# Gated delta rule in four chunks of 128 tokens, with a seventh level of the triangular inverse

## The reference

```
a_mat = where(tril_strict, (k*beta) @ k.T * decay, 0)        # inside one chunk
t_mat = inverse(eye + a_mat)                                 # unit lower triangular
u = t_mat @ (v*beta);  w = t_mat @ (k*beta*exp(gcum))
attn = where(tril, q @ k.T * decay, 0)
for each chunk:                                              # one after the other
    v_new = u - w @ state
    o     = (q*exp(gcum)) @ state + attn @ v_new
    state = state * exp(g_last) + k_tail.T @ v_new
```

## Time and profile before

| | |
|---|---|
| timed runs, median (lowest to highest) | 2641.55 us (2640.49 to 2644.19), 3 runs |
| profiled execution, span from first to last instruction | 2636.5 us; the profile gives no other time of it |
| PE busy | 97% of the span, 15565 MATMUL instructions |
| DVE, ACT, POOL busy | 49%, 24%, 12% |
| one chain (pair i = 1) | 500.30 to 591.80 us, 91.5 us |
| the four chains | 409.0 to 777.5 us |

### The profile page before, as it was taken

The page is one execution under the profiler, slowest core; times in us unless marked ns, Lnnn a source line. Parts: engine busy times, 40 slices in busy tenths (PEclk is TensorE's granted clock), DMA queues, the critical chain, the costliest instruction groups (busy, mean ns, idle before and its releaser), DMA issues.

```text
span 2636.5 us, 38190 instructions
## 1 busy us (share of the span) xinstructions
PE 2565.0 (97%) x15565; PEld 1758.4 (67%) x15565; DVE 1289.6 (49%) x2857; ACT 628.8 (24%) x1152; POOL 323.4 (12%) x315
## 2 busy tenths in 40 slices
PE   8999989999999999999999999999999999999998
PEld 4777757887885745444444446688864575888887
DVE  2255665766641012000024945676765665777733
ACT  1146543323321213011011144212110022121201
POOL 0222124444442400000001000000000000000000
PEclk9999999999999999999999999999999999999999
DMA  5211111111113222444423110222223212222222
GB/s 196 77 52 49 50 63 50 45 38 50 50 49 128 94 79 82 173 172 163 162 77 128 52 61 33 87 81 88 88 96 112 96 35 80 81 96 80 88 88 80
DMA packets 32519, 227.39 MB, mean 86 GB/s; under 512 B 3552, under 2 KB 4192, under 8 KB 6112
## 3 DMA queue, kind: packets, MB, share of 16 engines
q1 hardware_dynamic: 30384, 219.50, 23.7%
q10 hardware_dynamic: 1968, 5.51, 0.6%
HBM read 222.90 MB, written 2.10 MB: 85 GB/s over the span
## 4 chain that ended last, share of the span: by engine, by line
PE 92%; DVE 4%; ACT 2%; issue 1%; POOL 0%; DMA 0%; ACTq 0%; DVEq 0%; POOLq 0%
PE psum L404 90%; PE psum L902 1%; DVE work L1602 0%; PE psum L2810 0%; PE psum L1251 0%; POOL ring L1444 0%; PE psum L2471 0%; ACT work L2864 0%; DVE work L1055 0%; DMA mixT<-x_dram 0%; PE psum L3908 0%; PE psum L2146 0%; PE psum L1994 0%; DVE mixT L1147 0%; ACT work L968 0%
## 5 line engine op out<-in xcount | busy, mean ns | idle before, releaser
L404 PE MATMUL psum<-hT,ring 128*128 128x256 f32 (+2 forms) x2872 | 542.7, 369 | 8.4 <-issue 3.7
L404 PEld LDWEIGHTS psum<-hT,ring 128*128 128x128 f32 (+1 forms) x2872 | 373.5, 161 | 138.5 <-issue 96.7
L404 PE MATMUL psum<-work,ring 128*128 128x512 f32 (+1 forms) x1176 | 404.9, 496 | 5.3 <-ACT work L3736 2.4
L404 PEld LDWEIGHTS psum<-work,ring 128*128 128x128 f32 x1176 | 221.7, 190 | 168.7 <-issue 146.6
L404 PE MATMUL psum<-xT,ring 128*128 128x256 f32 (+2 forms) x1184 | 293.0, 398 | 8.4 <-ACT work L1384 4.3
L404 PE MATMUL psum<-work,mixT 128*128 128x256 f32 (+2 forms) x1332 | 289.3, 379 | 1.2 <-DVE mixT L3951 0.7
L404 PE MATMUL psum<-work 32*32 32x32 f32 (+8 forms) x5126 | 263.0, 247 | 13.7 <-issue 10.3
L404 PEld LDWEIGHTS psum<-work,mixT 128*128 128x128 f32 (+1 forms) x1332 | 232.1, 182 | 47.6 <-issue 16.4
L404 PEld LDWEIGHTS psum<-work 32*32 32x32 f32 (+3 forms) x5126 | 208.9, 123 | 75.4 <-issue 55.8
L404 PEld LDWEIGHTS psum<-xT,ring 128*128 128x128 f32 (+1 forms) x1184 | 209.8, 187 | 62.0 <-issue 25.1
L404 PE MATMUL psum<-ring,work 128*128 (+1 forms) x568 | 247.0, 593 | 0.6 <-DVE work L3031 0.6
(11 more groups left out here) (477 smaller groups left out, 2772.3 us busy)
## 6 DMA issues: line engine op xcount, KB each, us to landing
ring<-stream_dram SPq DMA_DIRECT2D x204, 1024.0 KB, 4.8
con<-consts_dram SPq DMA_DIRECT2D x1, 2953.0 KB, 13.5
mixT<-x_dram ACTq DMA_DIRECT2D x4, 512.0 KB, 6.4
work<-x_dram ACTq DMA_DIRECT2D x4, 512.0 KB, 6.4
out_dram<-mixT SPq DMA_DIRECT2D x4, 512.0 KB, 3.5
work<-p_dram ACTq DMA_DIRECT2D x1, 512.0 KB, 4.2
con<-ssm_dram ACTq DMA_DIRECT2D x1, 512.0 KB, 3.6
vec<-vecs_dram SPq DMA_DIRECT2D x1, 378.0 KB, 5.6
```

The costliest lines, as they stand in the source:

```text
L404: ins = self.eng.matmul(out, lhsT, rhs, start=start, stop=stop)
```

## The change

The chunk gets 128 tokens, so that a block of 128 holds one chunk. The masks, the running sum and the last decay of a chunk follow from the constant. The loop has 4 rounds instead of 8. All products in it have 128 columns. A seventh level (n = 6) joins the two halves of 64 rows of a block, with products of 64 x 64 by 64 columns (`half_ax`, `half_prod`), four for each head in each of its two bursts. For it level 5 also makes the lower left part of the plain (not transposed) inverse of the upper half: four more products a head on one 32 x 32 tile. `own_blocks` has three more small steps a head, `update` at level 5 one more. The projection products are dealt out anew: 5 and 4 in level 6, 4 before chunk 0, then 5, and 3 and 4 in each half of chunks 1 and 2, 112 as before. `u` now begins after product 88 and chunk 0 after product 92. On ACT `split_last_act` goes ahead of the SiLU of tile K0. On DVE the two halves of a tap tile stand before and behind each state.

```diff
-DH, DD, CH = 8, 128, 64
+DH, DD, CH = 8, 128, 128
@@ Chain, Pair
+                self.half_ax, self.half_prod = (self.A[:, 2 * P * n:2 * P * n + 2 * P].rearrange("p (b n) -> p b n", b=NB)
+                                                for n in range(2))
+                self.half_x = [self.vT[:, s, 2 * P:4 * P].rearrange("p (b n) -> p b n", b=NB) for s in range(2)]
+        CHUNKS, LEVELS = T // CH, 7
+        UPPER, LOWER = slice(0, 64), slice(64, P)
@@ chain_pe, level 5 and after it
+                        for b in range(NB):
+                            e.mm(by_part(h.x_prod)[PARTS[1], b, :], d.xt[s][PARTS[1], b, :], d.prod[s][PARTS[1], b, :])
                         ins = part_pairs(e, h.prod_xt, lambda b, lo, hi: (lo, d.prod[s][hi, b, :], d.xt[s][hi, b, :]))
...
             for s, h in enumerate(H):
                 e.eng.wait_ge(S["xt"], level_nth(i, 5, s))
+                for b in range(NB):
+                    ins = e.mm(h.half_ax[LOWER, b, :], blk(h.aT, b)[UPPER, LOWER], d.half_x[s][UPPER, b, :])
+                ins.then_inc(S["ax"], 1)
+            split.some(e, 5)
+            for s, h in enumerate(H):
+                e.eng.wait_ge(S["prod"], level_nth(i, 6, s))
+                for b in range(NB):
+                    ins = e.mm(h.half_prod[UPPER, b, :], d.half_x[s][LOWER, b, :], blk(h.xinvT, b)[LOWER, LOWER])
+                ins.then_inc(S["prod_xt"], 1)
+            split.some(e, 4)
+            for s, h in enumerate(H):
+                e.eng.wait_ge(S["xt"], level_nth(i, 6, s))
                 four(e, h.A, lambda b: (blk(h.xinvT, b), blk(h.v_b, b))).then_inc(S["u"], 1)
...
-            for c in range(T // CH):
+            for c in range(CHUNKS):
...
-                        e.mm(h.A[:, 0:P], blk(h.wT, b), h.state).then_inc(S["w_state"], 1)
-                        e.mm(h.B[:, at], h.state, h.qdT[:, at], True, False)
-                    if c < 7:
-                        split.some(e, 2)
+                        e.mm(h.A[:, 0:P], blk(h.wT, c), h.state).then_inc(S["w_state"], 1)
+                        e.mm(blk(h.B, c), h.state, blk(h.qdT, c), True, False)
+                    if c < CHUNKS - 1:
+                        split.some(e, 3)
...
-                if c < 7:
-                    split.some(e, 4 if c == 0 else 2)
+                if c < CHUNKS - 1:
+                    split.some(e, 5 if c == 0 else 4)
@@ chain_act
+            split_last_act(e, i + 1, K1)
             if more:
                 tapped_act(e, i + 1, K0)
-            split_last_act(e, i + 1, K1)
@@ chain_dve: product, update, own_blocks
+                    ins = nc.vector.tensor_copy(d.half_x[s][LOWER, :, :], h.half_ax[LOWER, :, :])
...
+                    nc.vector.tensor_scalar(d.half_x[s][PARTS[1], :, PARTS[0]], by_part(h.x_prod)[PARTS[1], :, :], -1.0, None, ALU.mult)
...
+                    ins = nc.vector.tensor_scalar(by_block(h.xinvT)[UPPER, :, LOWER], h.half_prod[UPPER, :, :], -1.0, None, ALU.mult)
...
+                nc.vector.memset(d.half_x[s][PARTS[0], :, PARTS[1]], 0.0)
+                for r in PARTS[0:2]:
+                    nc.vector.tensor_copy(d.half_x[s][r, :, r], d.x[s][r, :, :])
@@ chain_dve: the loop over chunks
+                if c == CHUNKS - 1:
+                    continue
+                if more:
+                    tapped_dve(e, i + 1, (V0, K1, V1)[c], 0, 2)
 ...
-                if more and c < 6:
-                    tapped_dve(e, i + 1, (V0, K1, V1)[c // 2], 2 * (c % 2), 2 * (c % 2) + 2)
+                if more:
+                    tapped_dve(e, i + 1, (V0, K1, V1)[c], 2, 4)
```

More of the change, by code:

```diff
@@ L1219, in level_nth, with state_nth @@
         def level_nth(i, n, s):
-            return (6 * i + n) * 2 + s + 1
+            return (LEVELS * i + n) * 2 + s + 1
         def chunk_nth(i, c, s):
-            return (T // CH * i + c) * 2 + s + 1
+            return (CHUNKS * i + c) * 2 + s + 1
+        def state_nth(i, c, s):
+            return ((CHUNKS - 1) * i + c) * 2 + s + 1
         def tapped(i, t):
@@ L1683, in chain_pe @@
             split.some(e, 4)
-            for c in range(T // CH):
-                b, lo = c // 2, (c % 2) * CH
-                r = slice(lo, lo + CH)
-                at = slice(CH * c, CH * c + CH)
+            for c in range(CHUNKS):
                 if c > 0:
@@ L1692, in chain_pe @@
                             e.eng.wait_ge(S["qd"], nth(i, s))
-                        e.eng.wait_ge(S["state"], chunk_nth(i, c - 1, s) - 2 * i)
-                        e.mm(h.A[:, 0:P], blk(h.wT, b), h.state).then_inc(S["w_state"], 1)
-                        e.mm(h.B[:, at], h.state, h.qdT[:, at], True, False)
-                    if c < 7:
-                        split.some(e, 2)
+                        e.eng.wait_ge(S["state"], state_nth(i, c - 1, s))
+                        e.mm(h.A[:, 0:P], blk(h.wT, c), h.state).then_inc(S["w_state"], 1)
+                        e.mm(blk(h.B, c), h.state, blk(h.qdT, c), True, False)
+                    if c < CHUNKS - 1:
+                        split.some(e, 3)
                 for s, h in enumerate(H):
@@ L1702, in chain_pe @@
                         e.eng.wait_ge(S["attn"], nth(i, s))
-                    if c < 7:
-                        e.mm(h.A[:, P:2 * P], blk(h.k_tail, b), v).then_inc(S["k_vnew"], 1)
-                    ins = e.mm(h.B[:, at], v, blk(h.attnT, b)[:, r], c == 0, True)
-                    if c == T // CH - 1:
+                    if c < CHUNKS - 1:
+                        e.mm(h.A[:, P:2 * P], blk(h.k_tail, c), v).then_inc(S["k_vnew"], 1)
+                    ins = e.mm(blk(h.B, c), v, blk(h.attnT, c), c == 0, True)
+                    if c == CHUNKS - 1:
                         ins.then_inc(S["o_whole"], 1)
-                if c < 7:
-                    split.some(e, 4 if c == 0 else 2)
+                if c < CHUNKS - 1:
+                    split.some(e, 5 if c == 0 else 4)
         def delta_pe(e):
@@ L1871, in product @@
                     ins = nc.vector.tensor_tensor(d.prod[s], by_part(h.ax), bc1(C("level")[:, 32 * n:32 * n + 32], NB), ALU.mult)
-                else:
+                elif n == 5:
                     for hi in PARTS[1::2]:
                         ins = nc.vector.tensor_copy(d.prod[s][hi, :, :], by_part(h.ax)[hi, :, :])
+                else:
+                    ins = nc.vector.tensor_copy(d.half_x[s][LOWER, :, :], h.half_ax[LOWER, :, :])
                 ins.then_inc(S["prod"], 1)
@@ L1919, in chain_dve @@
                 nc.vector.tensor_tensor(d.xt[s], bc1(C("eye32"), NB), by_part(h.prod_xt), ALU.subtract).then_inc(S["xt"], 1)
-            for n in range(1, 6):
+            for n in range(1, LEVELS):
                 for s, h in enumerate(H):
@@ L1951, in chain_dve @@
                         e.eng.wait_ge(S["u_out"], nth(i, s))
-                        nc.vector.tensor_copy(h.vnew[r, 0, :], blk(h.u, b)[r, :]).then_inc(S["vnew"], 1)
+                        nc.vector.tensor_copy(h.vnew[:, 0, :], blk(h.u, 0)).then_inc(S["vnew"], 1)
                     else:
-                        e.eng.wait_ge(S["w_state"], (7 * i + c - 1) * 2 + s + 1)
-                        nc.vector.tensor_tensor(h.vnew[r, c % 2, :], blk(h.u, b)[r, :], h.A[r, 0:P], ALU.subtract)\
+                        e.eng.wait_ge(S["w_state"], state_nth(i, c - 1, s))
@@ L1956, in chain_dve @@
+                        nc.vector.tensor_tensor(h.vnew[:, c % 2, :], blk(h.u, c), h.A[:, 0:P], ALU.subtract)\
                             .then_inc(S["vnew"], 1)
[L1957 to L1967, removed]
@@ L1968, in chain_dve @@
-                if more and c < 6:
-                    tapped_dve(e, i + 1, (V0, K1, V1)[c // 2], 2 * (c % 2), 2 * (c % 2) + 2)
+                if c == CHUNKS - 1:
+                    continue
+                if more:
+                    tapped_dve(e, i + 1, (V0, K1, V1)[c], 0, 2)
+                for s, h in enumerate(H):
+                    e.eng.wait_ge(S["k_vnew"], state_nth(i, c, s))
+                    if c == 0:
+                        ins = nc.vector.tensor_copy(h.state, h.A[:, P:2 * P])
+                    else:
+                        e.eng.wait_ge(S["state"], state_nth(i, c - 1, s))
+                        ins = nc.vector.scalar_tensor_tensor(out=h.state, in0=h.state,
+                                                             scalar=h.eg[:, CH * c + CH - 1:CH * c + CH],
+                                                             in1=h.A[:, P:2 * P], op0=ALU.mult, op1=ALU.add)
+                    ins.then_inc(S["state"], 1)
```

6 lines of the change are left out of this document (3 added, 3 removed).

## The result

The changed kernel takes 2624.17 us (median of 4 executions, 2619.89 to 2626.36); the kernel before took 2641.02 beside it (4 executions, 2635.05 to 2644.19). The ratio is 0.994, with a 95% interval of 0.9925 to 0.9955: 0.6% faster. The profiled execution has a span of 2624.5 us and took 2626.36, so 1.9 us lie around the span; 12.0 us of it are gone from the span of before (2636.5).

The account below looks back on a forecast made before the run. PE, busy 97% of the span, was taken as the bound. A pair: -7.2 + 0.6 + 2.4 + 2.2 = -2.0; four pairs -8.0, plus 1.5 for DVE waits, gives -6.5 us: 2641.55 to 2635, range 2627 to 2644.

Parts of the forecast that it names:

- Removed: 32 products of 0.225 a pair: Loop over chunks on PE: 13 products a head instead of 29, so 7.2 us less a pair.
- Level 5, 0.6 a pair: PE, 8 added products a pair on one 32 x 32 tile at 0.075 each: 0.6 us, bounds 0.2 to 1.8.
- Level 6, 2.4 a pair: PE, 16 products of 0.125 a pair plus 0.4 for changes of array shape: 2.4 us, bounds 1.6 to 4.0.
- The wait at product 92, 2.2 a pair in all four: Ahead of chunk 0, PE waits for POOL's sum, queued behind ACT's copies of `u` and `w`: 2.2 us, bounds 1.5 to 3.0.
- DVE, +0.5 in three pairs: PE waits for DVE 0.3 us after level 5's `update` and 0.2 us for taps at the loop's end, in three pairs.
- The base: Starting time: profiled span 2636.5 us to about 2630; median 2641.55, with 5 us more around it, to 2635.
- PE's "issue" gaps stay as they are: Four chains: 11.1 us in 8 PE gaps without known releaser; the forecast sum had no term for them.
- Rival (c): Added small bursts: PE runs short of instructions, one more 2.7 us gap a pair, +4.3 to +6.4 us in all; chance 0.12.

Follow-up runs that it names:

- second profile: Both kernels run and profiled again with no edit: the kernel before 1.0005, the changed kernel 0.9946 of the kernel before.
- shift of 128: 128 PE instructions (32 one-column products) added at the start of `load_pe` in both kernels: before 0.9943, changed 0.9933 of the unshifted kernel before.
- shift 0: Both kernels with no PE instructions added at the start: before 1, changed 0.9946 (five rounds).
- 64: 64 PE instructions (16 one-column products) added at the start of both kernels: before 0.9934, changed 0.9951 of the unshifted kernel before.
- 192: 192 PE instructions added at the start of both kernels: before 0.9964, changed 0.9937 of the unshifted kernel before.
- sixteen traces: All profiles of this case: both kernels, repeats, and follow-up kernels with shifted lists, ACT's copy moved or only the loop's part; ratios 0.9885 to 1.0005.
- four shifted forms: The kernel before with 64, 128, 192 or 256 PE instructions added at its start: 0.9934, 0.9943, 0.9964 and 0.9986.
- four starts: Each kernel with 0, 64, 128 and 192 PE instructions added at its start: mean ratio 0.9960 before, 0.9942 changed, 0.9901 changed with ACT's copy moved ahead.
- shift of 256: 256 PE instructions (64 one-column products) added at the start of the kernel before: 0.9986 of it unshifted.

## Why the prediction was wrong

The prediction's mechanism held and its sum nearly did; the step that failed is one that has no term in it. Its own steps, in order:

- *Removed: 32 products of 0.225 a pair.* Held. The half-rounds of after follow each other without holes, 2.19 us from 577.52 to 579.71 where half a round of four products (0.90) and three projection products (1.29) stand (weight loads of after):

```profile
577.52 0.41 PEld L404 LDWEIGHTS psum<-work 128*128 128x128 f32 x2
...
579.71 0.41 PEld L404 LDWEIGHTS psum<-work 128*128 128x128 f32 x2
```

- *Level 5, 0.6 a pair.* Too high: 24 products in 0.84 us where 16 took 0.63 is 0.21, the lower bound. The rule of 0.075 for each product on one tile, got from bursts that were spread evenly, didn't hold for a burst that is longer on one tile. Four pairs: 1.6 us of the miss.
- *Level 6, 2.4 a pair.* Held: 1.07 for 8 products is 0.13 each (0.125 taken), and 0.2 for the change of shape. The loads start 0.058 apart (16 from 561.03 to 561.90, two a product), all on one row group. The Trainium skill ("TensorE: Matmul & The Clock Gate", section "Part 3: Packing small matmuls") has such loads wait for the products in flight; a load of 53 ns by that page and a product taken to be as long, one behind the other, would put these rows 0.107 apart (an estimate from the page). The trace doesn't agree: 0.058.
- *The wait at product 92, 2.2 a pair in all four.* Held: 574.14 - 570.82 = 3.32, less 1.29 for three products, is 2.0; PE idle 1.8, four times. Taking away its cause ended the four waits, 7.1 us of idle PE, where 8.4 had been forecast.
- *DVE, +0.5 in three pairs.* About right, and small: at `half_ax` the products of the two heads stand apart in two pairs, so that the burst takes 1.37 and 1.46 us where it takes 1.14 in the others (the second profile shows 0.5 us of idle PE there in one pair). Beside this PE waits 0.4 us at level 5's last burst in one pair (in all four at a shift of 128, 1.5 in all), and at the end of the last pair 2.0 instead of 1.2. No wait on taps is seen at the end of the loop.
- *The base.* Taken as 5 us between the span and the median, from two numbers that belonged to different executions. Where an execution's span and time are both known, 1.9 lie between.
- *What was taken for granted: that PE's "issue" gaps stay as they are.* This failed. In the span they went from 15.2 to 6.7 us, 8.5 us for which the sum has no term. Rival (c) had them, as "the gaps, never explained", and asked only whether new bursts would add some. They hang on the count of instructions ahead of them. The edit shortened the list by 128 and so moved every seam behind the chains by half a piece, to the end of the kernel.

The terms for the chains, then: -6.5 as forecast, -1.6 for level 5, -4.4 for the gaps (11.1 to 6.7), and +1.7 for the clock. For the last, the windows of before and then of after (columns PE, its clock, DMA share, GB/s):

```profile
412.00:502.00 90.00, 85.97 (x1374) 0.98 0.14 47
502.00:593.00 91.00, 88.83 (x1396) 1.00 0.14 48
```

```profile
412.00:502.00 90.00, 84.53 (x1370) 0.98 0.14 48
502.00:593.00 91.00, 87.24 (x1381) 0.98 0.14 48
```

A mean of 0.98 over 90 us is a stretch at the lower level, 1.2 GHz, which costs about 1.7 us. Before had one, behind the gap of 2.1 us at 457 us; after has that one, behind 1.5 us at 456, and one more in pair 1, behind 1.8 at 552. Together -10.8, and -10.6 was measured. At a shift of 128, with as much of gaps in both and no such stretch, the same sum is -6.5 - 1.6 + 1.1 (for the waits at level 5's last burst, three more than at shift 0), so -7.0, against -5.9.

So near a sum as the first is in part luck, as the other pairs of profiles show. Take the chains from the first 32x32 product of pair 0 to their end as above, and from the difference of the two kernels the difference of the gaps and half of the time at the lower clock:

| pair of profiles | before, after | of it gaps | of it clock | left |
|---|---|---|---|---|
| shift 0 | 367.2, 356.7 | -4.4 | +1.7 | -7.8 |
| shift 0, second profiles | 368.9, 356.6 | -5.0 | -1.8 | -5.5 |
| 64 | 355.1, 356.2 | +4.1 | +3.4 | -6.4 |
| 128 | 355.7, 350.1 | -0.1 | 0 | -5.5 |
| 192 | 359.1, 352.3 | -0.3 | 0 | -6.5 |

What is left is the work and the waits: 5.5 to 7.8 us, mean 6.3, where the forecast is 6.5. Level 5's 1.6 us seem to be given back in small waits and in level 6 (2.54 for 2.4).

Behind the chains come -4.7 us for the untouched stage, 3.7 of them its two gaps, and +3.3 at 1000 to 1050. The latter is a clock again; windows of after:

```profile
1000.00:1030.00 30.00, 30.00 (x99) 17.53 (x98) 4.43 (x24) 13.72 (x47) 0.00 (x0) 0.89 0.03 7
```

0.89 over 30 us is some 6.6 us at the lower level, with PE busy all the time and no gap of PE ahead of it; the kernel before with a shift of 128 has 1.00 in this window. Nine of the sixteen traces show such a stretch there: eight of the ten with the new chunks, and one of the two profiles of the kernel before, where none of its four shifted forms has it. What starts it stays open.

So of the 12.0 us of the span, 6 to 8 come from the work and the waits that the prediction counted, and the rest is the balance of gaps and clock. Over four starts the change is worth about 5 us, give or take 2.5; the 6.5 of the forecast lies within that. A forecast's sum can be right and its time wrong, and that was missed: the range should have held a term for the gaps, up to the 15 us that the kernel has of them and down below nothing, and both ways.

## What to carry to other kernels

Before a change of less than 1% is believed, on an engine whose list is long, look whether the profile has idle time with no releaser ("issue") and whether the edit changes the number of that engine's instructions: if so, time both versions with the list shifted by a quarter, a half and three quarters of a piece, and compare the means. Choosing the best shift is a free edit (0.6% here), but it has to be chosen anew after every other one. Where a new layout brings a consumer nearer to a chain of engines that work in order, count that chain from the end that is fixed, and move the first link ahead of what it doesn't need: one line in ACT's order gave 11 us over four starts, 7 of them the wait itself, twice what the whole change did.

## What the hardware showed that was not expected

- PE's instructions come in pieces of 16.4 KB, 256 instructions, and the seams are not free. All 121 gaps of the sixteen traces stand at them. In the kernel before they cost 15.2 us in 11 gaps of up to 2.7, all in or right behind runs of small products; a run of 128 rows with their products, 256 instructions, takes 1.23 us. That a new piece takes longer to come than such a run takes to be worked off fits both numbers, but no run measured it by itself. The Trainium skill ("Runtime: NRT & Kernel Launch", section "Instruction fetch mechanics") says that instructions come in blocks of 256, which the packets and the shift of 256 bear out, and that fetching them is mostly hidden; at these bursts the trace doesn't agree.
- Behind such a gap the clock can fall. Behind the one of 2.1 us at 457, before has a mean of 0.83 over 10 us, which is 3.4 us at the lower level, so the gap costs 1.7 more than it shows.

```profile
455.00:465.00 10.00, 7.96 (x182) 6.34 (x182) 2.96 (x13) 0.60 (x1) 1.86 (x2) 0.83 0.03 7
```

  The length of the gap doesn't decide it: behind those of 2.7 us at 643 and 736 in the same trace the clock stays at 1.00, and in the second profile it falls behind the one at 735 (2.9 us). What does stays open.

- Products of 64 x 64 on one tile take 0.13 us each, between 0.225 for 128 x 128 and, for 32 x 32, 0.02 spread over four tiles (64 in 1.27), 0.04 over two (16 in 0.63) and 0.03 for the eight added on one (0.21).
